# Block scores, spread sample values, and carried states in the weight ring

## The reference, cut to what matters

```
b = cumsum(log_a)                                   # inside a chunk
scores[t,s] = sum_d q[t,d] k[s,d] exp(b[t,d]-b[s,d])   for s <= t
o = scores @ v + (q*exp(b)) @ S
S = exp(b_last)*S + (k*exp(b_last-b)).T @ v         # new state
o = rms_norm(o) * w * silu(gate)
```

## Time and profile before

| what | value |
|---|---|
| median of 3 runs (lowest, highest) | 1896.83 us (1892.1, 1898.84) |
| the profiled execution | 1899.02 us; span 1897.0 us |
| busy: PE, PEld, DVE, ACT, POOL | 1494.9, 814.1, 425.3, 262.8, 118.9 us |
| DMA | 535.04 MB, mean 282 GB/s |
| chain that ended last | PE 52%, DMA 25%, SP's queue 11%, DVE 9% |
| mixer of layer 0 | from 127.4 to 208.9 us |
| mixer of layer 1 | from 1046.9 to 1162.3 us |

### The profile page before, as it was taken

One profiled execution on the slowest core, in us unless ns is written; L12 is line 12 of the kernel. 1 busy time (PEld: TensorE's weight loads), 2 busy tenths in 40 slices (PEclk: granted clock), 3 DMA queues, 4 the chain that ended last, 5 costly groups with the idle time before them and its releaser, 6 DMA issues.

```text
span 1897.0 us, 19986 instructions
## 1 busy us (share of the span) xinstructions
PE 1494.9 (79%) x8254; PEld 814.1 (43%) x8254; DVE 425.3 (22%) x931; ACT 262.8 (14%) x510; POOL 118.9 (6%) x238
## 2 busy tenths in 40 slices
PE   8998899968867776677599888999778677666773
PEld 6767466645312222122275664666453122222220
DVE  0338420151111100111410663201411111011104
ACT  1233101210000000000122321012100000000000
POOL 3113020000000000000010320200000000000000
PEclk9996799976988988888799767999869898888987
DMA  9432344863999999999923222547729999999993
GB/s 343 140 134 71 102 159 178 331 268 148 409 409 410 409 410 410 409 410 409 348 89 133 92 95 85 185 180 292 306 109 409 409 410 410 409 410 410 409 410 124
DMA packets 164424, 535.04 MB, mean 282 GB/s; under 512 B 5326, under 2 KB 22798, under 8 KB 161808
## 3 DMA queue, kind: packets, MB, share of 16 engines
q1 hardware_dynamic: 160448, 519.98, 70.8%
q0 software_dynamic: 2192, 7.98, 1.3%
q10 hardware_dynamic: 1728, 6.29, 0.9%
HBM read 521.75 MB, written 12.49 MB: 282 GB/s over the span
## 4 chain that ended last, share of the span: by engine, by line
PE 52%; DMA 25%; SPq 11%; DVE 9%; issue 1%; ACT 1%; DVEq 0%; ACTq 0%; POOL 0%
PE ps L553 12%; SPq L369 10%; DMA scr<-in_w_gate 10%; DMA W<-in_w_gate 7%; PE ps L815 7%; PE ps L798 7%; PE ps L598 6%; DMA W<-in_w_down 4%; PE ps L581 3%; PE ps L587 3%; DMA scr<-in_w_down 3%; PE ps L687 2%; PE ps L568 2%; DVE scr L1185 2%; DMA scr<-in_w_up 1%
## 5 line engine op out<-in xcount | busy, mean ns | idle before, releaser
L815 PE MATMUL ps<-W,scr 128*32 128x512 f32 x2304 | 319.9, 698 | 136.5 <-DMA W<-in_w_gate 87.0
L553 PE MATMUL ps<-XT,W 128*128 128x288 f32 x896 | 225.3, 415 | 3.0 <-ACT XT L919 2.8
L815 PEld LDWEIGHTS ps<-W,scr 128*32 128x32 f32 x2304 | 72.2, 121 | 347.2 <-issue 162.9
L553 PEld LDWEIGHTS ps<-XT,W 128*128 128x128 f32 x896 | 173.6, 195 | 53.3 <-ACT XT L919 4.1
L815 PE MATMUL ps<-scr 128*32 128x512 f32 x768 | 126.1, 792 | 86.6 <-DMA scr<-in_w_gate 37.3
L1380 DVE TENSOR_TENSOR scr<-scr,ps 128x512 f32<-128x512 f32 x16 | 11.0, 688 | 751.2 <-PE ps L815 751.2
L798 PE MATMUL ps<-scr,X 128*128 128x128 f32 (+1 forms) x864 | 171.6, 332 | 9.2 <-DVE scr L1348 9.2
L798 PEld LDWEIGHTS ps<-scr,X 128*128 128x128 f32 (+1 forms) x864 | 132.3, 208 | 67.8 <-issue 29.4
L815 PEld LDWEIGHTS ps<-scr 128*32 128x32 f32 x768 | 25.0, 132 | 175.5 <-DMA scr<-in_w_gate 55.8
L781 PE MATMUL ps<-scr 128*128 128x512 f32 x144 | 73.9, 619 | 3.9 <-ACT scr L1078 2.3
L598 PE MATMUL ps<-W,scr 128*128 128x512 f32 x128 | 60.4, 632 | 9.6 <-DVE scr L1213 9.6
(11 more groups left out here) (282 smaller groups left out, 1434.0 us busy)
## 6 DMA issues: line engine op xcount, KB each, us to landing
W<-in_w_gate SPq DMA_DIRECT2D x48, 2048.0 KB, 23.6
W<-in_w_up SPq DMA_DIRECT2D x48, 2048.0 KB, 23.8
W<-in_w_down SPq DMA_DIRECT2D x48, 2048.0 KB, 23.8
scr<-in_w_up SPq DMA_DIRECT2D x16, 2048.0 KB, 23.5
scr<-in_w_gate SPq DMA_DIRECT2D x16, 2048.0 KB, 23.6
scr<-in_w_down SPq DMA_DIRECT2D x16, 2048.0 KB, 23.9
W<-in_cache_mem_k SPq DMA_DIRECT2D x8, 2048.0 KB, 9.3
W<-in_cache_mem_v SPq DMA_DIRECT2D x8, 2048.0 KB, 8.3
```

The costliest lines, as they stand in the source:

```text
L553: last = mm(bank[:, 0:NT], w[:, k, c * P:(c + 1) * P], XT[:, k, :], start=(k == 0), stop=(k == KC - 1))
L815: last = mm(ps[j * CAP:(j + 1) * CAP, bank, :], x[:, k, j * CAP:(j + 1) * CAP], w[:, j, a, :], start=(k == 0), stop=(k == x.shape[1] - 1))
```

## The change

It has four parts, all in the mixers.

1. **Block scores.** The six lowest levels (`CL` = 6, blocks of up to 32 tokens) are formed only inside the diagonal 32x32 blocks: 48 small products for both prompt tiles, all in bank 0, with the sample scores beside them. DVE multiplies once by a compact mask (128x384), sums the 6 levels once, and spreads the sums over the four blocks of a row (zeros elsewhere). The two upper levels need no mask: six products into bank 4, which ACT copies straight into `st`.
2. **Spread sample values.** POOL spreads the values by sequence (`vx`, 32 x 8 nv) in place of the key tokens; the new sample states are then 2 products (layer 1: 4) of 512 columns with the key tokens as weights. They go to banks 1, 2 (layer 1: 1, 3, 2, 7).
3. **States through the ring.** One more unit (layer 1: two) carries all heads' sample states into `W`; DVE updates them there, SP writes a head out when it is done, from rows that lie together in memory (the kernel's arrays for the states are laid out so). The slots are free when all heads have been written out. SP's state sequence stands ahead of unit `S0 + 6`, which is mv1 in layer 0 and mv0 in layer 1. `sf` has two buffers.
4. **Order.** PE no longer waits for `rms` of the head before ahead of the key transposes, only ahead of the output products. POOL starts the exponents after `ktok_ps`, not after the state update. ACT takes the exponentials for head h + 2 at the end of head h (for head 1: inside head 0, after the upper copies).

```diff
+            CL, BLK, UPPER = 6, 32, 96
+            for j in range(DVC[l]):
+                units.append((l, f"S{j}", carried[:, j * KC * HALF:(j + 1) * KC * HALF]...))
@@ SP
-                        for h in range(HEADS):
...
-                            sp.dma_start(s_out[h][:, late], s0[:, late])...
-                            sp.dma_start(s0[:, late], s_in[h + 1][:, late])...
+                    if n == UNIT[l, "S0"] + SLOTS:
+                        for h in range(HEADS):
+                            sp.wait_ge(S("state_new"), count_at("state_new", l, h + 1))
+                            sp.dma_start(s_out[:, h * per:(h + 1) * per], carried_state(l, h)...)
+                            sp.dma_start(p_out[h], m["sf"][:, h % 2, :])...
@@ POOL
                     if h >= 2:
-                        pool.wait_ge(S("state_new"), count_at("state_new", l, h - 1))
+                        pool.wait_ge(S("ktok_ps"), count_at("ktok_ps", l, h - 1))
...
+                def spread_values(h):
+                    if h:
+                        pool.wait_ge(S("ns_ps"), count_at("ns_ps", l, 2 * DVC[l] * h))
...
+                    st.tell(tt(m["vx"]..., m["v"][0:NS, PT_:PT_ + 1, h * nv:(h + 1) * nv].to_broadcast([NS, DB, nv]),
+                               bmask[0:NS].unsqueeze(2).to_broadcast([NS, DB, nv]), ALU.mult), S("vx"))
@@ PE
                     pe.wait_ge(S("qk_ready"), count_at("qk_ready", l, h + 1))
+                    for lv in range(CL):
+                        for t in range(PT_):
+                            at = (lv * PT_ + t) * BLK
+                            for j in range(P // BLK):
+                                c = slice(t * P + j * BLK, t * P + (j + 1) * BLK)
+                                score(lv, c, c, ps[j * BLK:(j + 1) * BLK, 0, at:at + BLK])
+                    for lv in range(SL):
+                        last = score(lv, cols(PT_), cols(PT_), ps[0:NS, 0, at:at + NS])
+                    last.then_inc(S("score_ps"), 1)
+                    if h: pe.wait_ge(S("ms_ready"), count_at("ms_ready", l, h))
+                    for t in range(PT_):
+                        score(7, ..., ps[0:2 * BLK, 4, at:at + 2 * BLK])
+                        for j in range(0, P // BLK, 2):
+                            score(6, left, right, ps[j * BLK:(j + 1) * BLK, 4, at + 2 * BLK:at + UPPER])
                     pe.wait_ge(S("kd_ready"), count_at("kd_ready", l, h + 1))
-                    if h:
-                        pe.wait_ge(S("rms"), count_at("rms", l, h))
...
+                    pe.wait_ge(S("so_ready"), count_at("so_ready", l, h + 1))
+                    pe.wait_ge(S("up_ready"), count_at("up_ready", l, h + 1))
+                    pe.wait_ge(S("s1_ready"), count_at("s1_ready", l, h + 1))
+                    if h: pe.wait_ge(S("rms"), count_at("rms", l, h))
...
                     last.then_inc(S("o_ps"), 1)
-                    for b in range(DB):
-                        last = mm(ps[:, b // per, ...], m["kexp"][:, b, :], m["v"][0:NS, 2, h * nv:(h + 1) * nv], ...)
+                    pe.wait_ge(S("vx"), count_at("vx", l, h + 1))
+                    new_part(0); new_part(1)       # ktok weights, 512 columns of vx
+                    if l:
+                        new_part(2)
+                        pe.wait_ge(S("sf_ready"), count_at("sf_ready", l, h + 1))
+                        new_part(3)
                     pe.wait_ge(S("sq_ready"), count_at("sq_ready", l, h + 1))
@@ ACT
-                    if h + 1 < HEADS:
-                        decays(h + 1)
+                    act.wait_ge(S("st_ready"), count_at("st_ready", l, h + 1))
+                    fn(m["st"][0:2 * BLK, 0:PT_, 2 * BLK:P], above[0:2 * BLK, :, 0:2 * BLK], ACT.Copy)
+                    ...                            # two more copies
+                    if h == 0:
+                        decays(1)
...
                     fetch_table(ACT.Exp)
+                    if h + 2 < HEADS:
+                        decays(h + 2)
@@ DVE
-                    for t in range(TT):
...
-                        step(tt(ms, src, masks[0:R, 0:L, 0:C], ALU.mult))
-                        tell(red(m["st"][0:R, t, 0:C], ms.rearrange("p l t -> p t l"), AX.X, ALU.add), S("st_ready"))
+                    dve.wait_ge(S("score_ps"), count_at("score_ps", l, h + 1))
+                    tt(m["cs"], ps[:, 0, 0:CL * PT_ * BLK], cmask[:], ALU.mult)
+                    step(tt(m["ss"][0:NS], ps[0:NS, 0, ...], cmask[0:NS, :]..., ALU.mult))
+                    red(m["st"][0:NS, PT_, 0:NS], m["ss"][0:NS]..., AX.X, ALU.add)
+                    step(red(m["sums"]..., m["cs"].rearrange("p (v x) -> p x v", v=CL), AX.X, ALU.add))
+                    for t in range(PT_):
+                        ins = tt(m["st"][:, t, :]..., bc(m["sums"][:, t:t + 1, :], ...), bc(blocks[:].unsqueeze(2), ...), ALU.mult)
+                    tell(ins, S("st_ready"))
+                    tell(stt(m["sf"][:, h % 2, :], m["s1"], dec[:, 1:2], ps[:, 7, nv:2 * nv], ALU.mult, ALU.add), S("sf_ready"))
                     if h + 1 < HEADS:
                         decayed(h + 1)
```

More of the change, by code:

```diff
@@ L59, in build @@
     SL = 3
+    CL = 6
+    BLK = 32
+    UPPER = 3 * BLK
     MT_ = MEM // P
@@ L83, in build @@
         ones = sb("ones", [P, P])
-        masks = sb("masks", [P, LEVELS, P])
-        ident = masks[:, 0, :]
+        ident = sb("ident", [P, P])
+        cmask = sb("cmask", [P, CL * 2 * BLK])
+        blocks = sb("blocks", [P, P // BLK])
         fold = sb("fold", [P, NS])
@@ L153, in build @@
             if l == 0:
-                m["conv"] = [r.take(CW // P, NT) for _ in range(3)]
                 r.at = mark
                 m["up"], m["us"] = r.take(CW // P, SEQ + 2), r.take(CW // P, DB, 6)
+                m["conv"] = [r.take(CW // P, NT) for _ in range(3)]
             MIX.append(m)
@@ L319, in used @@
                     sp.wait_ge(S("mix_unit"), 2 * i + int(name[-1]) + 1)
+                elif name[0] == "S":
+                    for parity in range(2):
+                        sp.wait_ge(S(f"state_out{parity}"), count_at("state_out", l, 32 * (HEADS // 2)))
                 elif name[0] == "K":
@@ L406, in _ @@
                                        pattern=[[1, P]], channel_multiplier=-1), S("consts"))
-            for lv in range(1, LEVELS):
+            for lv in range(1, CL):
                 B = 1 << lv
-                right = masks[:, lv, :].rearrange("p (n two h) -> p n two h", two=2, h=B // 2)[:, :, 1, :]
+                right = built[:, lv - 1, :].rearrange("p (n two h) -> p n two h", two=2, h=B // 2)[:, :, 1, :]
                 one = ones[:].rearrange("p (n two h) -> p n two h", two=2, h=B // 2)[:, :, 1, :]
@@ new lines, in mixer @@
+                    for t in range(PT_):
+                        ins = tt(m["st"][:, t, :].rearrange("p (j c) -> p j c", c=BLK), bc(m["sums"][:, t:t + 1, :], P, P // BLK, BLK),
+                                 bc(blocks[:].unsqueeze(2), P, P // BLK, BLK), ALU.mult)
+                    tell(ins, S("st_ready"))
+                    if h >= 2:
+                        dve.wait_ge(S(f"state_out{h % 2}"), count_at("state_out", l, 32 * (h // 2)))
+                    dve.wait_ge(S("s_ps"), count_at("s_ps", l, h + 1))
@@ L1424 @@
             a = a.reshape(d, b, m, h, 2, 128).transpose(0, 1, 5, 3, 4, 2).reshape(d, b, 128, 2 * h * m)
+        elif name in ("state_hgrn", "state_gla"):
+            a = a[0].transpose(2, 1, 0, 3).reshape(a.shape[3], -1)
         elif name == "mem_prompt":
```

191 lines of the change are left out of this document (98 added, 93 removed).

## The result

Four runs of the changed kernel took 1850.2 to 1854.05 us, median **1851.39 us**, beside 1894.74 us for the kernel before in the same job: ratio 0.9771, 95% interval [0.9747, 0.9795]. The forecast was 1884 us with a range from 1862 to 1903.

A forecast was written before the change was run, and what follows sets the result against it. Weights were taken to pace the expert stages, so microseconds saved in the mixer heads' chain of waits count in the time. Layer 0's 7.9 and layer 1's 5.3 us made 13 off 1896.8: 1884 us, range 1862 to 1903.

The forecast's parts named there:

- the first sentence on the bound: Expert stages: weights set the pace and the change touches nothing there; 0 us saved.
- main case: Whole kernel: mixers shorter at the low clock, 13 us off, 1884 us, own range 1876 to 1892; chance 0.43.
- The sum: Mixers only: layer 0 saves 7.9 us and layer 1 5.3, together 13 us off the median of 1896.8.
- Second and third heads: Middle heads of each mixer: cycles of 17.5 us for 20.0 in layer 0, 26.7 for 29.1 in layer 1.
- The inner terms: Within a cycle: blocks 2.9 us, key tokens at 5.4, ScalarE free at 4.9, new-state products 3.45 and 6.85.
- Last heads: Last head of each layer: priced like the heads before it, 17.5 us in layer 0 and 26.7 in layer 1.
- First head of layer 1: Layer 1's first head: 0.7 us lost, as products that ran at the full clock may not.
- A: Mixers: the full clock comes back; cycles 16.2 and 24.7 us, 1871 us, or 1839 with all products full; chance 0.23.
- B: TensorE's block scores: half the pace at the low clock, 60 ns a pass, 17 us more, 1901 us; chance 0.14.
- C: TensorE's block scores: blocks go one after another, about 107 ns each, 50 us more, 1932 us or so; chance 0.08.
- the row of 30 ns: TensorE's block scores: priced from 64 passes in four column groups, 1.93 us; 30 ns a pass, 2.9 us.
- D: Mixer chain: DVE's products late beside POOL, or mv1 late behind states; half the saving used up, 1890 to 1893; chance 0.12.

The follow-up runs named there:

- a_pad32: The changed kernel with 32 unused bytes per partition ahead of W, so that W starts at byte 21536; 1876.42 us, ratio 0.9898.
- a_pad64: The changed kernel with 64 unused bytes per partition ahead of W, so that W starts at byte 21568; 1874.49 us, ratio 0.9897.

## Why the prediction was wrong

*The step that failed* is the first sentence on the bound: the expert stages are where "the weights set the pace and the change touches nothing". The weights do set the pace; but the change moved their target by 2016 bytes, and the place of that target alone is worth 19 us in the kernel before and 25 in the kernel after; in the two traces the expert stages are 22 us shorter. With `W` off its multiple (`a_pad32`) the change comes to 1876.4 us, on the edge of the main case's own range. The sum had no term for it, and no rival did.

*Second and third heads: right.* 17.5 and 26.7 us were forecast; 17.4 and 16.9, and 26.7 twice, were measured. The 16.9 came with a part of the full clock, 0.60; in `a_pad32`, at 0.50, that head takes 17.4 too. The output products start 9.15 and 11.1 us into the cycle, for 9.5 and 11.4 (the prediction's own terms add up to 9.35 and 11.25). The inner terms were less good. Blocks take 1.5 us for 2.9, but the copy of the key tokens is at 4.85 for 5.4, not sooner in proportion, since ScalarE is free only at 4.85; the forecast had its end at 4.9. The new-state products kept 3.71 and 7.12 us; the 0.26 for weight loads did not come.

*Last heads: too dear.* All heads were priced with four exponentials between root and key tokens and at the low clock; the last has no exponentials there, and in both layers a part of it ran at the full clock. 15.9 for 17.5 and 24.3 for 26.7, and 0.6 in the third head of layer 0: 4.6 us in all. In `a_pad32`, at 0.50 throughout, layer 0's last head takes 16.4, so 1.1 of its 1.6 us are there without the clock and 0.5 came with it. Layer 1's last head was at 0.64 in that trace too, so there the two are not separated.

*First head of layer 1: wrong sign.* It gained 4.1 us where 0.7 was to be lost. The chain of the kernel before has, there too,

```profile
1049.01 1.24 DVE scr L1184
...
1050.27 1.93 DVE scr L1185
...
1053.49 1.94 DVE scr L1185
...
1056.04 0.49 PE ps L675 x2
```

DVE's 7.0 us of masks and sums between scores and output products, as in every other head: in layer 1 the saving was counted in the later heads only. Nor did the clock fall earlier than before: it is 1.00 up to 1034, 11 us into the head, and was 0.91 from 5 to 11 us into it before and 0.50 from there. PE in the timeline after, same head:

```profile
1029.69 0.46 PE L711 MATMUL ps<-scr 128*128 128x128 f32 x2 [1.70 <-ACT scr L1029]
...
1033.07 3.94 PE L700 MATMUL ps<-scr 32*128 32x512 f32 x8
...
1036.94 2.29 PE L729 MATMUL ps<-scr,ones 128*128 128x288 f32 x4
```

The output products start 7.0 us into the head for 9.2 before, 2.2 earlier, without the two long DVE sums. From there to the end of the squares it takes 9.5 us for 14.8, most of it at the full clock (the new-state products 3.9 for 7.1). But the squares, done at 1039.2, are scaled at 1042.72 only: 3.5 us of these 7.5 are lost to DVE, which is late with the decayed keys and queries beside POOL's exponents and so with the state update. In layer 0's first head those fifteen products take from 133.8 to 140.3, 6.5 us for the 3.5 of before, and its squares, done at 139.3, are scaled at 142.51; it gained 0.5 us, for 0.4. Among the fifteen products those of 128 columns start some 0.41 us apart while POOL's exponents run, and 0.20 apart in the kernel before.

These two items, 4.6 and 4.8, are nearly all of the mixers' 9.6 beyond the forecast. Of the 1.8 us ahead of the first mixer, 1.6 lie in the first 64 products of the input projection (18.8 us before, 17.2 after). With the same instructions the traces of the kernels above have 17.2 (`a_pad64`) to 18.8 (`a_pad32`), whatever the address, so the change is not shown to have given them.

*The rivals.* A came in part: the clock is full for some of the third and last heads (0.56 to 0.64 for 0.50) and of layer 1's first, not in the second. B and C fell with the 16 ns a pass and the doubled blocks. Here the row of 30 ns, too, was an upper end: it has 128 columns, and a pass of 32 took 11 ns at the full level (96 from 125.58 to 126.6) and 16 at the low one. The rule of the Trainium skill weighed in the prediction ("TensorEngine Tiling (Array Packing)", Instruction Overhead: about 60 cycles for each product, so that few columns gain nothing) does not hold for passes that go round four column groups: at 1.2 GHz it would be 50 ns by estimate, and the measurement decides. D came in the first heads alone, where DVE's products are late beside POOL and the squares wait more than 3 us to be scaled; in the later heads they are covered. Its other half did not come: the value products of layer 0 follow the key products at 257.75 without a wait for mv1.

## What to carry to other kernels

A diff also changes what it does not mention: where every later tensor lies. Before calling a stage untouched, compare the tensors' addresses, and read its rate in GB/s, not its busy tenths. When heads of a loop are priced by the middle one, price the first and the last by their own chains, and compare heads of two kernels at like clocks. And before an edit takes work out of a chain by reordering, see what the same engine then covers less.

## What was not expected of the hardware

The experts' transfers, 2 MB from HBM into a 16 KB row of each partition, ran at 420 GB/s in these kernels when the rows of `W`, three in four of their targets, started on a multiple of 256 bytes of the partition (21504, 21760, 23552), at 410 when they started 32, 64 or 224 bytes beyond one (21536, 21568, 23520), and at 421 to 422 with the fourth on a multiple as well. A packet of 4096 bytes took 159.5 to 159.6, 163.7 to 163.9 and 159.0 ns. The Trainium skill, "DMA: Bandwidth & Descriptors", "How a descriptor splits into AXI transactions", has the unit of 256 bytes for the side that is read; in these runs the side read was the same, and it shows on the side that is written.
